# Inverse roots of the retention norm formed as a power on GpSimd instead of a root on ScalarE and a reciprocal on VectorE

## The reference

```python
def rms_norm(x, g=None):
    xf = x.astype(jnp.float32)
    y = xf * lax.rsqrt(jnp.mean(jnp.square(xf), axis=-1, keepdims=True) + EPS)
    ...

def ret_output(o, g):
    b, s = o.shape[:2]
    return rms_norm(o).reshape(b, s, RET_HEADS * RET_DV).astype(g.dtype) * jax.nn.silu(g)

def layer(x, c, l, mixer):
    ...
    x = gated_post(x, swiglu(h, ffn_w1[l, 0], ffn_w3[l, 0], ffn_w2[l, 0]), norm_post[l, 0], mods, 0, 0.5)
    h = modulated_pre(x, norm_pre[l, 1], mods, 1)
    o, st = mixer(h, l)          # attention | ret_output(retention), times w_out
    ...
```

## Time and profile before

| | us |
|---|---|
| median of three runs | 2586.87 |
| lowest and highest of the three | 2583.16, 2590.44 |
| the profiled execution | 2585.33 |
| its span | 2583.3 |
| PE busy in the span | 2378.5 (92%) |
| DVE busy | 1308.3 (51%) |
| POOL busy | 862.0 (33%) |
| ACT busy | 811.9 (31%) |

### The profile page before, as it was taken

The page is one execution under the profiler, slowest core; times in us unless marked ns, Lnnn a source line. Parts: engine busy times, 40 slices in busy tenths (PEclk is TensorE's granted clock), DMA queues, the critical chain, the costliest instruction groups (busy, mean ns, idle before and its releaser), DMA issues.

```text
span 2583.3 us, 43948 instructions
## 1 busy us (share of the span) xinstructions
PE 2378.5 (92%) x17558; PEld 2238.5 (87%) x17558; DVE 1308.3 (51%) x2006; ACT 811.9 (31%) x1365; POOL 862.0 (33%) x366
## 2 busy tenths in 40 slices
PE   1999999899888899999989999889988898999996
PEld 1999989898456899999989999889965588999996
DVE  7333379775473333337253335986935515333552
ACT  1322222433233432322242232224323334323221
POOL 0334334343000433434433433443420033343342
PEclk9999999999999999999999999999999999999998
DMA  6222267323100222226312224761221011222551
GB/s 221 74 85 85 92 228 275 125 82 106 47 1 1 66 82 85 86 94 234 130 56 90 81 89 150 271 233 58 81 79 33 1 49 58 89 81 89 183 194 57
DMA packets 71507, 272.48 MB, mean 105 GB/s; under 512 B 8640, under 2 KB 10048, under 8 KB 70528
## 3 DMA queue, kind: packets, MB, share of 16 engines
q1 hardware_dynamic: 71424, 271.35, 31.1%
HBM read 267.87 MB, written 3.45 MB: 105 GB/s over the span
## 4 chain that ended last, share of the span: by engine, by line
PE 77%; DVE 10%; issue 5%; ACT 3%; DMA 2%; POOL 1%; DVEq 0%; SPq 0%; ACTq 0%
PE ps L515 22%; PE ps L516 21%; PE ps L519 21%; PE ps L525 2%; PE ps L809 2%; PE ps L853 1%; DVE ret_q L1379 1%; DVE ret_k L1379 1%; PE ps L805 1%; POOL w_lo L440 1%; PE ps L538 1%; DVE wide_v L1228 1%; PE ps L540 1%; PE ps L719 1%; DMA raw<-in_w_mix 1%
## 5 line engine op out<-in xcount | busy, mean ns | idle before, releaser
L440 POOL TENSOR_TENSOR w_lo<-raw,w_hi 128x1024 fp32r<-128x1024 f32 (+1 forms) x304 | 789.7, 2598 | 1660.6 <-ACT w_hi L925 1293.7
L515 PE MATMUL ps<-h_hi,w_hi 128*128 128x274 f32 x3296 | 897.4, 289 | 9.2 <-DVE z_tmp L1348 5.4
L516 PE MATMUL ps<-h_lo,w_hi 128*128 128x274 f32 x3296 | 900.7, 290 | 0.0
L519 PE MATMUL ps<-h_hi,w_lo 128*128 128x274 f32 x3296 | 686.0, 289 | 0.0
L515 PEld LDWEIGHTS ps<-h_hi,w_hi 128*128 128x128 f32 x3296 | 626.8, 190 | 12.0 <-issue 6.7
L516 PEld LDWEIGHTS ps<-h_lo,w_hi 128*128 128x128 f32 x3296 | 620.8, 188 | 0.2
L925 ACT CAST w_hi<-raw 128x1024 fp32r<-128x1024 f32 (+1 forms) x236 | 268.9, 1139 | 886.0 <-PE ps L519 710.4
L519 PEld LDWEIGHTS ps<-h_hi,w_lo 128*128 128x128 f32 x3296 | 520.3, 188 | 0.0
L515 PE MATMUL ps<-u_hi,w_hi 128*128 128x272 f32 x1408 | 383.5, 291 | 15.5 <-POOL w_lo L440 15.5
L516 PE MATMUL ps<-u_lo,w_hi 128*128 128x272 f32 x1408 | 380.8, 288 | 0.0
L1228 DVE CUSTOM_DVE_ANT_0 wide_v<-ada_w,ps 128x1024 bf16<-128x1024 f32 x288 | 332.1, 1218 | 45.7 <-DMA ada_w<-in_ada 29.5
(11 more groups left out here) (215 smaller groups left out, 2526.6 us busy)
## 6 DMA issues: line engine op xcount, KB each, us to landing
raw<-in_w_up SPq DMA_DIRECT2D x176, 512.0 KB, 3.3
ada_w<-in_ada SPq DMA_DIRECT2D x160, 512.0 KB, 4.7
raw<-in_w_dn SPq DMA_DIRECT2D x64, 704.0 KB, 5.0
raw<-in_w_mix SPq DMA_DIRECT2D x64, 512.0 KB, 3.3
decay<-in_decay SPq DMA_DIRECT2D x2, 2048.0 KB, 8.2
x<-in_x SPq DMA_DIRECT2D x1, 2176.0 KB, 9.0
rope_tab<-in_rope SPq DMA_DIRECT2D x2, 1088.0 KB, 4.8
out_y<-x SPq DMA_DIRECT2D x1, 2176.0 KB, 7.3
```

What stands on the lines that cost most here:

```text
L440: pool.tensor_tensor(w_lo[:, slot, 0:width], raw[:, slot, 0:width], w_hi[:, slot, 0:width].bitcast(F32), ALU.subtract).then_inc(lo_done.se ...
L515: pe.matmul(ps[:, bank + t, 0:half], wh, hi[:, n], start=start, stop=False)
L516: pe.matmul(ps[:, bank + t, 0:half], wh, lo[:, n], start=False, stop=False)
L519: last = pe.matmul(ps[:, bank + t, 0:half], wl, hi[:, n], start=False, stop=stop)
```

## The change

ACT's instruction in `norm_root` now only scales and adds eps (`Identity` in place of `Sqrt`), so `ret_root` receives the mean square plus eps. POOL raises each of the four tiles in place to the power -0.5, as a `tensor_tensor` with a column of -0.5 spread over the 544 columns. The four instructions stand in POOL's queue after the subtraction for the second output chunk and before that for the third. DVE multiplies `ret_v` by the tile that POOL wrote; its reciprocals and the waits around them go. In all there are four powers, four reciprocals and four roots per layer, in two layers.

```diff
+        minus_half = sb("minus_half", [P, 1])
...
         @block.gpsimd
         def _(pool):
+            pool.memset(minus_half[:, :], -0.5).then_inc(half_set.sem, 1)
+            pool.wait_ge(half_set.sem, 1)
...
-                with pool.Fori(2, (OUT_C0 + 4) // 2) as i:
+                with pool.Fori(2, (OUT_C0 + 2) // 2) as i:
                     for k in range(2):
                         low(l, MIX_C0 + i * 2 + k, k, KD * P)
+                for n in range(4):
+                    pool.wait_ge(m_root.sem, m_root.at(l, 2 + n + 1))
+                    pool.tensor_tensor(ret_root[:, n, :], ret_root[:, n, :], minus_half[:, :].to_broadcast([P, T]), ALU.pow)\
+                        .then_inc(ret_inv.sem, 1)
+                for k in range(2):
+                    low(l, MIX_C0 + OUT_C0 + 2 + k, k, KD * P)
                 add_first_squares(l, 1)
...
-                    nc.scalar.activation(halves(ret_root[:, n, :]), pair(4 + 2 * (n % 2)), ACT.Sqrt,
+                    nc.scalar.activation(halves(ret_root[:, n, :]), pair(4 + 2 * (n % 2)), ACT.Identity,
                                          bias=eps[:, 0:1], scale=1.0 / VD).then_inc(m_root.sem, 1)
...
                 def ret_prods(n):
-                    dve.wait_ge(m_root.sem, m_root.at(l, 2 + n + 1))
-                    if n:
-                        dve.wait_ge(ret_prod.sem, ret_prod.at(l, 2 * n))
-                    v_.reciprocal(rinv[:, :], ret_root[:, n, :]).then_inc(m_inv.sem, 1)
-                    dve.wait_ge(m_inv.sem, m_inv.at(l, 2 + n + 1))
-                    v_.tensor_tensor(ret_v[:, n, :], ret_v[:, n, :], rinv[:, :], ALU.mult).then_inc(ret_prod.sem, 1)
+                    dve.wait_ge(ret_inv.sem, ret_inv.at(l, n + 1))
+                    v_.tensor_tensor(ret_v[:, n, :], ret_v[:, n, :], ret_root[:, n, :], ALU.mult).then_inc(ret_prod.sem, 1)
                     dve.wait_ge(ret_prod.sem, ret_prod.at(l, 2 * n + 1))
                     v_.tensor_tensor(ret_v[:, n, :], ret_v[:, n, :], ret_g[:, n, :], ALU.mult).then_inc(ret_prod.sem, 1)
```

More of the change, by code:

```diff
@@ L261, in streaming_trunk @@
         m_root = signal("m_root", 6)
-        m_inv = signal("m_inv", 6)
+        m_inv = signal("m_inv", 2)
+        ret_inv = signal("ret_inv", 4)
+        half_set = signal("half_set", 0)
         q_scaled = signal("q_scaled", 2)
```

## The result

The changed kernel takes 3171.2 us, the median of 4 runs (3168.35 to 3173.62), where the kernel before took 2588.6 on the same chip (2583.16 to 2590.44). The ratio is 1.2253, with a 95% interval of 1.2233 to 1.2272. The forecast was 2659 us with a range of 2574 to 2781: the sign came out, the size did not. The time lies far outside the range.

A forecast was written before the change was run, and what follows sets the result against it. The attention was taken as bound by no single engine, with two of four reciprocals on the chain. Delay 4X - 7.4 less gains 3.86 and 0.88 gave 35.9 us per layer at X = 12.0: 2659 us, range 2574 to 2781.

The forecast's parts named there:

- The duration of a power: POOL's power over 128 x 544 was estimated at 12.0 us, between 1.4 and 27.3, from DVE's reciprocal.
- The rival of the slow software: On POOL, lanes or steps of a power run one after another: above 27 us each, time above 2781; chance 0.10.
- X: Duration of one power on POOL over a 128 x 544 tile, taken as 12.0 us.
- The shut-out: Powers on POOL hold out DVE's masked keys for their whole length, delaying PE's first score by 4X - 7.4 us per layer.
- the formula 2563 + 8X: Forecast time of the whole changed kernel under the shut-out, written 2587 - 24 + 8X; 2659 us at X = 12.0.
- a power, whose time is arithmetic, does not hold DVE out: Rival: POOL's powers stay out of DVE's way; full 11.0 us gain, 2576 us, up to X = 12.7; chance 0.12.
- The two rivals: Slow software on POOL (X above 27 us, chance 0.10) and powers staying out of DVE's way (2576 us, chance 0.12).
- The table load, 0.76: Dropping ACT's 1.28 us load before the first root saves PE 0.76 us per layer waiting for copied queries.
- The first reciprocal, 3.86: Between PE's first transposes of item 0 and its next scores, 3.86 us per layer saved, partly through the clock.
- The fourth, 0.88: Dropping the fourth reciprocal saves 0.88 us per layer between PE's sample scores and its transposes.
- The second and third, zero: These reciprocals on DVE lie beside PE's scores and values, off the chain, so removing them gains zero.
- The sum, 5.50 per layer: Gains in the attention from table load and reciprocals, 0.76 + 3.86 + 0.88 = 5.50 us per layer, 11.0 in all.

The follow-up runs named there:

- e1_mult: Changed kernel with POOL's four powers per layer replaced by four multiplications of the same tiles (power left out); 2580.28 us, ratio 0.998 to the kernel before.
- e10_long: Changed kernel with one POOL multiplication over all four tiles (2176 columns) after the fourth scaling instead of the powers; 2586.26 us, ratio 0.9996 to the kernel before.
- e7_cols72: Changed kernel with each power over only the first 72 of 544 columns, others not raised; 2578.24 us, ratio 0.9971 to the kernel before.
- e2_none: Changed kernel without POOL's powers; DVE multiplies by ACT's mean square directly (inverse root left out); 2575.25 us, ratio 0.9966 to the kernel before.
- e3_sqrt_only: Kernel before without its four reciprocals per layer; root and table load stay (inverse left out); 2574.64 us, ratio 0.996 to the kernel before.
- e9_id_ln_exp: Changed kernel with powers replaced on ACT by one logarithm and one exponential over all four tiles, identity per tile kept; 2576.73 us, ratio 0.9956 to the kernel before.
- e6_forms: Changed kernel with its eight powers replaced by eight instructions of different exponent, base, columns and partitions, one a multiplication; run once, no total time given.
- e5_ln_exp: Changed kernel with powers replaced on ACT by a logarithm per tile instead of identity and one exponential over four tiles; 2578.63 us, ratio 0.9972 to the kernel before.

## Why the prediction was wrong, point by point

**The duration of a power: the step that failed first.** "1 + 2 x 3.9 = 8.8 passes, 8.8 x 1.363 = 12.0 us", with 27.3 as the upper end; it is 87.12. The step that failed is the carrying over of DVE's reciprocal: it took for granted that POOL makes a power in some number of passes like DVE's, and only asked how many. Measured is the time of 64 passes, so twenty were no bound either. The rival of the slow software, with X above 27 and a time above 2781, got 0.10 and is what happened. No row of the trace before shows a function on POOL; where the nearest row is of another engine, the upper end should not have come from an idea of how it is written. The Trainium skill's rule (GPSIMD Engine Reference, section 7, Performance pitfalls) of 4 cycles per dependent fp32 step had given, with the twenty steps that I had assumed, an estimated 36 us and 2852 us; measured are 87.12 and 3171, so it pointed the right way, and rule and steps together were short by 2.4 times.

**The shut-out: failed as well, and on its own.** "An instruction of one that needs both holds out the other for its whole length." That holds for ordinary passes, also for the one-input keys (e1_mult, e10_long). It was carried over to powers and fails there: even with X = 12 the forecast of 2659 would have been wrong, as e7_cols72 shows with 2578; and with the measured X the formula 2563 + 8X would have given 3260, 89 us too long. I had called the alternative by its name, "a power, whose time is arithmetic, does not hold DVE out", and gave it 0.12.

**The two rivals together give the result.** Where powers stay out of DVE's way the time is 2576 us up to X = 12.7 and rises by 8 us for each further us of X (4 per layer): 2576 + 8 x (87.12 - 12.7) = 3171. Measured is 3171.2. The exact hit is partly luck: by this sum the stage should have grown by 4 x 74.4 - 5.5 = 292.2 us and grew by 290.7 including what follows it, and 4 us of the span lie elsewhere and are not explained. That the slope is right, two points show: from X = 22.04 to 87.12 the time over the kernel before on the same chip grows from 62.5 to 582.6 us, which is 8.0 us for each us of X. The third, X = 11.84, lies on the flat part, as it should.

**The gains.** *The table load, 0.76:* PE's idle time is gone, as said, but its first score comes 1.10 us earlier in e2_none than in e3_sqrt_only, since eight matmuls behind the stall take 1.28 us instead of 1.84 as well. *The first reciprocal, 3.86:* 2.29 in e3's trace. The failed part is the clock: I held that the value matmuls would come back to 2.47 us with the reciprocal gone; they stay at about 4.1 in e2, e3 and e9, and at 4.63 in the changed kernel, where the first product waits. *The fourth, 0.88:* right. *The second and third, zero:* some 0.25 together in e3's trace, not tried apart. *The sum, 5.50 per layer:* e2_none gained 6.05 in its trace, since the clock at item 0's scores rose instead (0.58 before, 1.00 in e2). Its median is 10.2 us below the kernel before, 5.1 per layer. The total was near, its parts were not.

**Sign and signs in the profile.** The chances for slower, 0.81, rested mostly (0.71 of it) on a hold that no power showed, so the right sign is partly luck: only the rival of 0.10 had slower for the reason that came about. The prediction had named what would prove it wrong, the keys at 0.48 us beside a power and PE waiting at the products, and both rows are there.

**Open.** Why a power costs 160 ns per column, and why a product of DVE is held only at its start. A packed layout was not tried: the mean square repeats over the 64 rows of a head, so the different values of a layer are 8 x 544, which fill 34 columns of 128 partitions; at 159.6 ns each and 0.3 us that would be an estimated 5.7 us for a layer, plus what packing and spreading cost. What sets the clock at item 0's scores, and why its value matmuls mostly stay at 1.2 GHz (0.66 granted around them in e2_none), no run settles.

## What to carry to other kernels

Before a function is moved to another engine, its duration there has to be measured: no row of an ordinary pass bounds it, here 64 times off, and one run of the instruction by itself would have shown it. When no row shows it, the time that the plan allows (here 12.7 us per power) is the number to compute first, since beyond it every us costs four per layer. And an engine that idles through a stage is not the best home for that alone: ACT made logarithm and exponential of all four tiles in 4 us, inside its own waits.

## What the runs showed of the hardware

- A power on POOL costs 159.6 ns per column and some 0.3 us, the same for the exponents -0.5 and 1, for a base of 1 and for 16, 64 and 128 partitions (e6_forms): 87.12 us for 544 columns.
- It keeps a two-input instruction of DVE that starts with it waiting only for some 1.6 ns per column (0.89, 0.44 and 0.21 us at 544, 272 and 136 columns); an ordinary pass of POOL holds DVE to its end (4.09 us over 2176 columns), one-input keys at the double rate too (e10_long).
- A product on POOL whose second input is one column broadcast takes 1.09 us over 128x544, against 1.36 with two full inputs.
- ACT's logarithm and exponential over 128x2176 take 2.0 us each. Going from the one function to the other cost a table load of 1.28 us, as did the first use of the logarithm; two exponentials in a row shared one load (e9_id_ln_exp).
- The twenty value matmuls of item 0 ran mostly at the lower clock (4.1 us against 2.47) behind an idle time of 1.74 us in PE, no longer than the 1.83 of the later item whose matmuls were fast; in the second layer of e5_ln_exp, behind 1.74 us again, they were fast (2.50) where the scores before them had been slower (15.45 us against 13.9).
